# Gated linear attention of the prompt: eight levels of masked pair products in place of sixteen lags and chunk states

## What is computed

```python
def gla_chunked(q, k, v, glog, s0):
    c = math.gcd(q.shape[1], GLA_CHUNK)
    causal = jnp.tril(jnp.ones((c, c), bool))[:, :, None]
    def step(S, inp):
        qc, kc, vc, gc = inp
        bcum = jnp.cumsum(gc, axis=2)
        diff = jnp.where(causal, bcum[:, :, :, None, :] - bcum[:, :, None, :, :], -jnp.inf)
        att = jnp.einsum('bhid,bhjd,bhijd->bhij', qc, kc, jnp.exp(diff))
        o = (jnp.einsum('bhij,bhjv->bhiv', att, vc)
             + jnp.einsum('bhid,bhdv->bhiv', qc * jnp.exp(bcum), S))
        b_last = bcum[:, :, -1:, :]
        S = (jnp.exp(b_last[:, :, 0, :, None]) * S
             + jnp.einsum('bhjd,bhjv->bhdv', kc * jnp.exp(b_last - bcum), vc))
        return S, o
```

## Time and profile before

| | us |
|---|---|
| median of 3 runs | 2249.26 |
| lowest, highest | 2247.94, 2251.69 |
| the profiled execution, its own time | 2248.67 |
| its span, first to last instruction | 2246.9 |
| mean granted TensorE clock | 0.893 |

### The profile page before, as it was taken

One profiled execution on the slowest core, in us unless ns is written; L12 is line 12 of the kernel. 1 busy time (PEld: TensorE's weight loads), 2 busy tenths in 40 slices (PEclk: granted clock), 3 DMA queues, 4 the chain that ended last, 5 costly groups with the idle time before them and its releaser, 6 DMA issues.

```text
span 2246.9 us, 26096 instructions
## 1 busy us (share of the span) xinstructions
PE 1998.4 (89%) x9816; PEld 1517.5 (68%) x9816; DVE 1487.3 (66%) x1522; ACT 996.3 (44%) x1033; POOL 254.4 (11%) x191
## 2 busy tenths in 40 slices
PE   5998678889998984787789999999999999999998
PEld 2784235679996752354667777777777778777776
DVE  1298463445554894534368788787877868788786
ACT  1211311234422213201057666676666667666664
POOL 1159400000002495000000000000000000000000
PEclk9895686799999966865879999999999999999999
DMA  9468473155507691441249899897997979899892
GB/s 366 173 256 291 187 263 123 60 166 180 181 19 283 232 360 38 188 161 67 75 160 362 299 341 341 300 355 293 341 343 284 357 279 355 298 347 345 290 365 110
DMA packets 238516, 552.21 MB, mean 246 GB/s; under 512 B 14792, under 2 KB 43632, under 8 KB 234096
## 3 DMA queue, kind: packets, MB, share of 16 engines
q1 hardware_dynamic: 224736, 475.96, 59.1%
q0 software_dynamic: 5920, 70.23, 8.0%
q10 hardware_dynamic: 7792, 5.08, 0.7%
HBM read 546.16 MB, written 5.08 MB: 245 GB/s over the span
## 4 chain that ended last, share of the span: by engine, by line
PE 46%; DVE 6%; issue 5%; ACT 3%; DVEq 0%; ACTq 0%
PE bank L787 12%; PE bank L789 11%; PE bank L788 11%; DVE WL L1628 2%; ACT WH L1532 2%; PE bank L755 2%; PE bank L1154 2%; PE bank L1076 1%; PE bank L1252 1%; PE bank L813 1%; PE bank L780 1%; PE bank L1006 1%; PE bank L978 0%; DVE Y L2098 0%; PE bank L805 0%
## 5 line engine op out<-in xcount | busy, mean ns | idle before, releaser
L1628 DVE TENSOR_TENSOR WL<-ring_low,WH 128x2048 fp32r<-128x2048 f32 x369 | 838.7, 2290 | 277.8 <-ACT WH L1532 195.2
L1532 ACT ACTIVATE WH<-ring_low 128x2048 fp32r<-128x2048 f32 x336 | 637.9, 1917 | 259.7 <-PE bank L789 259.7
L787 PE MATMUL bank<-WH,HGH 128*128 128x512 f32 x896 | 369.3, 412 | 16.3 <-DVE WL L1628 16.3
L789 PE MATMUL bank<-WH,HGL 128*128 128x512 f32 x896 | 350.5, 391 | 0.0
L788 PE MATMUL bank<-WL,HGH 128*128 128x512 f32 x896 | 349.9, 391 | 0.0
L787 PEld LDWEIGHTS bank<-WH,HGH 128*128 128x128 f32 x896 | 168.7, 188 | 59.7 <-DVE WL L1628 23.4
L787 PE MATMUL bank<-WH,ATH 128*128 128x512 f32 x448 | 186.8, 417 | 24.4 <-DVE ATL L1628 24.4
L789 PEld LDWEIGHTS bank<-WH,HGL 128*128 128x128 f32 x896 | 168.5, 188 | 36.6
L788 PEld LDWEIGHTS bank<-WL,HGH 128*128 128x128 f32 x896 | 168.9, 189 | 32.3
L788 PE MATMUL bank<-WL,ATH 128*128 128x512 f32 x448 | 181.4, 405 | 0.0
L789 PE MATMUL bank<-WH,ATL 128*128 128x512 f32 x448 | 180.8, 404 | 0.0
(11 more groups left out here) (364 smaller groups left out, 2819.5 us busy)
## 6 DMA issues: line engine op xcount, KB each, us to landing
ring_low<-moe_w SPq DMA_DIRECT2D x336, 1024.0 KB, 6.3
ring_low<-ffn_w SPq DMA_DIRECT2D x33, 1024.0 KB, 5.3
ring_low<-w_ada SPq DMA_DIRECT2D x16, 2048.0 KB, 15.3
ring_high<-w_ada SPq DMA_DIRECT2D x8, 2048.0 KB, 16.5
ring_low<-w_in SPq DMA_DIRECT2D x7, 2048.0 KB, 17.5
ring_low<-w_out SPq DMA_DIRECT2D x4, 2048.0 KB, 11.2
ring_high<-w_in SPq DMA_DIRECT2D x3, 2048.0 KB, 8.6
C<-consts SPq DMA_DIRECT2D x1, 1174.0 KB, 18.4
```

The source lines that it names most:

```text
L787: mm(out, sh, mh, start=start, stop=False)
L789: return mm(out, sl, mh, start=False, stop=stop)
L1532: A(WH[:, q % NSPLIT, :], eraw[q % NRAW], ACT.Copy).then_inc(high_ready, 1)
L1628: return tt_(out, full, high.bitcast(F32), ALU.subtract)
```

## The change

The prompt's GLA has no chunks any more. At level n the 256 tokens are taken as blocks of 2^(n+1); a pair (j, i) belongs to the level at which j lies in the left half and i in the right half of the same block. There the decay splits at the middle: the key side takes the gate sum from j to the end of the left half, the query side the sum from the middle to i. So each level needs one scaled copy of all keys and queries (`WX`, half of the tokens as keys, half as queries), and one product of keys with queries per head and tile of 128 tokens (`pair_products`: 8 matmuls with 64 rows and 128 by 128 outputs, half as many at level 7, which joins the two tiles). 0/1 masks keep the level's pairs: DVE copies the product into `ATT` where the mask is one (`keep_pairs`, two predicated copies a level). The pairs i = j come from `gd`, the plain product. `GSUM` (in place of the gates) is extended level by level: after level n the right half adds the left half's sum. It replaces the scan. The factor 1/16 moves into the exponentials' scale.

After level 7 the values meet the pair weights in 12 matmuls (`gy`), read by ACT into `O`. The end state is one token-major product of decayed keys and values (`gtk`, `gst`); values are turned before the levels (`gtv`). All of `VX`, the chunk states, their reads and the additions to `O` are gone.

The fills change: 'lag' is 14 and 8 steps before each of 8 levels (7 and 4 before each of 16 lags), 'kq' 8 and 8, 'gk' 8 and 16; 'vx' and 'states' are gone. The order of background steps is as before, so steps not placed here come in later fills. The core of the diff; a line of "..." also stands where lines of the kernel before, shown above, are taken out:

```diff
-CH = 16
-NCH = NP // CH
+LEVELS = 8
+LMASK = 7
...
+    j, i = np.arange(P)[:, None], np.arange(P)[None, :]
+    masks = [(j >> n + 1 == i >> n + 1) & (j >> n & 1 == 0) & (i >> n & 1 == 1) for n in range(LMASK)] + [i == j]
+    put('levels', np.ascontiguousarray(np.stack(masks, 1).astype(np.uint8)).reshape(P, -1).view(f))
...
-JOBS += [('gate0', 'v'), ('gate1', 'v')] + [(f'att{i}', 'v') for i in range(CH)]
-JOBS += [('gkv0', 'a'), ('gkv1', 'a'), ('gts', 'a')]
-JOBS += [(f'kv{_tt}{_pr}', 'v') for _tt in range(2) for _pr in range(2)]
-JOBS += [('gi0', 'v'), ('gi1', 'v'), ('gx0', 'v'), ('gx1', 'v'), ('gs0', 'v'), ('gs1', 'v'),
+JOBS += [('gate0', 'v'), ('gate1', 'v'), ('gtv0', 'a'), ('gtv1', 'a'), ('gts', 'a'), ('gd0', 'v'), ('gd1', 'v')]
+JOBS += [(f'lv{_n}{_s}', 'v') for _n in range(LMASK) for _s in range(2)]
+JOBS += [('lv70', 'a'), ('lv71', 'a')] + [(f'gy{_h}', 'a') for _h in range(NH)] + [('gtk0', 'a'), ('gtk1', 'a'), ('gst', 'a')]
+JOBS += [('gx0', 'v'), ('gx1', 'v'), ('gs0', 'v'), ('gs1', 'v'),
...
-        'sumb': (8, 0), 'mean': (8, 0), 'var': (0, 0), 'gate': (4, 0), 'lag': (7, 4), 'kq': (3, 7),
-        'vx': (8, 16), 'states': (8, 8), 'gx': (5, 8), 'gs': (4, 0), 'gn': (8, 9), 'rr': (0, 16),
+        'sumb': (8, 0), 'mean': (8, 0), 'var': (0, 0), 'gate': (4, 0), 'lag': (14, 8), 'kq': (8, 8),
+        'gk': (8, 16), 'gx': (5, 8), 'gs': (4, 0), 'gn': (8, 9), 'rr': (0, 16),
...
                 for tt in range(2):
...
+                    token_major(l, f'gtv{tt}', tt, (gv[:, 0, :], gv[:, 1, :]))
                 b = open_job(l, 'gts')
                 for n, src in enumerate((gk[:, 0, NP:T], gk[:, 1, NP:T], gv[:, 0, NP:T], gv[:, 1, NP:T])):
                     ins = turn(b[0:NS, n * P:(n + 1) * P], src, P)
                 close(ins)
+                def pair_products(name, keys, queries, tiles):
+                    for s in range(2):
+                        r = slice(s * HD, (s + 1) * HD)
+                        b = open_job(l, f'{name}{s}')
+                        for n, (kt, qt) in enumerate(tiles):
+                            for c in range(2):
+                                o = (2 * n + c) * P
+                                ins = mm(b[:, o:o + P], keys[r, c, kt * P:(kt + 1) * P],
+                                         queries[r, c, qt * P:(qt + 1) * P], start=True, stop=True)
+                        close(ins)
+                pe.wait_ge(ev["gla_q"], l + 1)
+                pair_products('gd', gk, gq, ((0, 0), (1, 1)))
+                for n in range(LEVELS):
+                    fill('lag')
+                    pe.wait_ge(ev["level_w"], l * LEVELS + n + 1)
+                    pair_products(f'lv{n}', WX[n % 2], WX[n % 2], ((0, 0), (1, 1)) if n < LMASK else ((0, 1),))
+                fill('kq')
+                for name in (f'lv{LMASK - 1}1', 'lv71'):
+                    who, count = read_no(l, name)
+                    pe.wait_ge(job_read[who], count)
+                for h in range(NH):
+                    c, s = h // 2, h % 2
+                    v = [TMV[:, tt, h * HD:(h + 1) * HD] for tt in range(2)]
+                    o = open_job(l, f'gy{h}')[s * HD:(s + 1) * HD, :]
+                    mm(o[:, 0:P], v[0], ATT[:, s, 0, c, :], start=True, stop=True)
+                    mm(o[:, P:NP], v[0], ATT_OFF[:, s, c, :], start=True, stop=False)
+                    close(mm(o[:, P:NP], v[1], ATT[:, s, 1, c, :], start=False, stop=True))
+                fill('gk')
+                pe.wait_ge(ev["gla_kq"], l + 1)
                 for tt in range(2):
...
+                    token_major(l, f'gtk{tt}', tt, (GKD[:, 0, :], GKD[:, 1, :]))
+                b = open_job(l, 'gst')
+                who, count = read_no(l, 'gtk1')
+                pe.wait_ge(job_read[who], count)
+                for h in range(NH):
+                    c, s = h // 2, (h % 2) * HD
+                    for tt in range(2):
+                        ins = mm(b[s:s + HD, c * HD:(c + 1) * HD], TMK[:, tt, h * HD:(h + 1) * HD],
+                                 TMV[:, tt, h * HD:(h + 1) * HD], start=(tt == 0), stop=(tt == 1))
+                close(ins)
...
+                A(GX[:, :, NP:T], GX[:, :, NP:T], ACT.Exp, scale=1.0 / 16.0).then_inc(ev["gla_decays"], 1)
                 for tt in range(2):
...
+                    read(A(TMV[:, tt, :], job(l, f'gtv{tt}')[:, 0:GW], ACT.Copy))
                 read(A(KV8[:, :], job(l, 'gts')[0:NS, :], ACT.Copy))
...
+                for n in range(LEVELS):
+                    rows(l, f'lv{n}1')
+                    act.wait_ge(ev["level_diff"], l * LEVELS + n + 1)
+                    e, g = halves(EX[n % 2], n), halves(GSUM, n)
+                    A(e[:, :, :, 0, :], e[:, :, :, 0, :], ACT.Exp, scale=1.0 / 16.0).then_inc(ev["level_exp"], 1)
+                    A(e[:, :, :, 1, :], g[:, :, :, 1, :], ACT.Exp, scale=1.0 / 16.0).then_inc(ev["level_exp"], 1)
+                act.wait_ge(ev["gla_kd"], l + 1)
+                A(GKD, GKD, ACT.Exp, scale=1.0 / 16.0).then_inc(ev["gla_kexp"], 1)
+                for s in range(2):
+                    read(A(ATT_OFF[:, s].rearrange("p c i -> p (c i)"), job(l, f'lv7{s}')[:, 0:NP], ACT.Copy))
+                for h in range(NH):
+                    c, s = h // 2, (h % 2) * HD
+                    read(A(O[s:s + HD, c, 0:NP], job(l, f'gy{h}')[s:s + HD, 0:NP], ACT.Copy))
+                for tt in range(2):
+                    read(A(TMK[:, tt, :], job(l, f'gtk{tt}')[:, 0:GW], ACT.Copy))
+                read(A(PT[:, P:2 * P], job(l, 'gst')[:, 0:P], ACT.Copy))
+                wait_read(l, 'gst')
+                store(act, gla_out[l, :, :, 0:HD], PT[:, P:2 * P].rearrange("p (c v) -> p c v", c=2))
...
+                signal(tt_(GX, GM, GA, ALU.subtract), "gla_b", l + 1)
                 gq = Z[:, ZT['gq']:ZT['gq'] + 2, :]
                 gk = Z[:, ZT['gk']:ZT['gk'] + 2, :]
...
                 wait_z(l, 'gv')
...
+                signal(ts(gq, gq, HD ** -0.5, None, ALU.mult), "gla_q", l + 1)
+                d.add(V.memset(ATT.rearrange("p s t c i -> p (s t c i)"), 0.0))
+                def difference(n):
+                    g = halves(GSUM, n)
+                    tt_(halves(EX[n % 2], n)[:, :, :, 0, :], bend(block_sum(n), 1 << n), g[:, :, :, 0, :],
+                        ALU.subtract).then_inc(ev["level_diff"], 1)
+                def weights(n):
+                    e, w = halves(EX[n % 2], n), halves(WX[n % 2], n)
+                    if n >= 2:
+                        dve.wait_ge(job_done, job_no(l, f'lv{n - 2}1') + 1)
+                    dve.wait_ge(ev["level_exp"], 2 * (l * LEVELS + n) + 2)
+                    d.add(tt_(w[:, :, :, 0, :], e[:, :, :, 0, :], halves(gk[:, :, 0:NP], n)[:, :, :, 0, :], ALU.mult))
+                    tt_(w[:, :, :, 1, :], e[:, :, :, 1, :], halves(gq[:, :, 0:NP], n)[:, :, :, 1, :],
+                        ALU.mult).then_inc(ev["level_w"], 1)
+                    d.wait()
+                    g = halves(GSUM, n)
+                    d(tt_(g[:, :, :, 1, :], g[:, :, :, 1, :], bend(block_sum(n), 1 << n), ALU.add))
+                def keep_pairs(name, n):
+                    mask = c_('levels', P, n * P // 4, (n + 1) * P // 4).bitcast(U8)
+                    for s in range(2):
+                        read(l, f'{name}{s}', V.copy_predicated(
+                            ATT[:, s].rearrange("p t c i -> p (t c) i"), bmid(mask, 4),
+                            job(l, f'{name}{s}')[:, :].rearrange("p (n i) -> p n i", n=4)))
+                for n in range(LEVELS):
+                    difference(n)
+                    if n == 1:
+                        d.wait()
+                        keep_pairs('gd', LMASK)
+                    elif n >= 2:
+                        keep_pairs(f'lv{n - 2}', n - 2)
+                    weights(n)
+                dve.wait_ge(k_stored, 16 * (l + 1))
+                signal(tt_(GKD, bend(GSUM[:, :, NP - 1], NP), GSUM, ALU.subtract), "gla_kd", l + 1)
+                keep_pairs(f'lv{LMASK - 1}', LMASK - 1)
+                dve.wait_ge(ev["gla_kexp"], l + 1)
+                signal(tt_(GKD, GKD, gk[:, :, 0:NP], ALU.mult), "gla_kq", l + 1)
+                wait_act_read(l, 'gts')
+                dve.wait_ge(job_done, job_no(l, 'lv71') + 1)
                 dve.wait_ge(ev["gla_decays"], l + 1)
...
                 dve.wait_ge(ev["gate_silu"], 3 * (l + 1))
+                wait_act_read(l, 'gy3')
```

More of the change, by code:

```diff
@@ L23 @@
 U32 = mybir.dt.uint32
+U8 = mybir.dt.uint8
 ALU = mybir.AluOpType
@@ L86 @@
                ('cos', T), ('sin', T),
-               ('reset', NP), ('slot', P), ('decay', NH * NP), ('causal', 3 * P),
-               ('chunk', 8), ('half', 2), ('dk', 2 * NH), ('gamma', 2), ('eio', NE)):
+               ('levels', (LMASK + 1) * P // 4), ('slot', P), ('decay', NH * NP), ('causal', 3 * P),
+               ('half', 2), ('dk', 2 * NH), ('gamma', 2), ('eio', NE)):
     CCOL[_k] = (_n, _w)
@@ L246, in host_constants @@
     put('causal', np.concatenate([tri, np.zeros((P, P), f), tri], 1))
```

(63 more changed lines are left out.)

89 lines of the change are left out of this document (10 added, 79 removed).

## The result

The changed kernel takes 2185.48 us (median of 4 runs, 2183.92 to 2187.88) against 2249.03 for the kernel before (4 runs): a ratio of 0.9717, 95% interval 0.9700 to 0.9734. It is 2.8% faster, where 2260, about 11 us slower, was forecast. The profiled execution's span is 2182.1 us, against 2246.9.

A forecast was written before the change was run, and what follows sets the result against it. PE's serial queue of weight-row fills and pair products bounds both stretches. Mostly at 1.2 GHz, layer 0 gives 0, layer 1 -3, later steps -9, overlap +1: about 11 us slower, 2260 us, range 2198 to 2280.

The forecast's parts named there:

- What bounds the stretches: In each layer's gated-attention stretch, PE's serial queue of fills and pair products sets the pace (91.4 and 104.0 us before).
- PE's bank: Sign inside the levels: DVE's idle time in the changed profile would be named after this; no size given.
- the 2.4 us behind ACT's row work: At a row's end, copy, exponentials, weights and hand-overs delay the next products by 2.4 us, with PE idle.
- The price of a set, P: Eight pair-product matmuls of one level on PE: 2.5 us at the full clock, 4.5 at the lower one.
- the isolated row: Trace row L1040, taken as the price of one pair-product matmul: 0.31 us at full clock, 0.56 at the lower.
- The twelve products with the values: PE matmuls behind the levels, priced at 12 x 0.56 = 6.7 us at the lower clock.
- The clock: Both stretches mostly at 1.2 GHz: layer 1 nearly all through, layer 0 a third of the time at 2.4.
- the first rival: Full clock holds in both stretches, 64-row matmuls counting like 128-row ones: 2200 us, faster; chance 0.24.
- Later steps: Weight-row steps issued later, behind the stretches: 5 us lost in layer 0, 4 in layer 1; 3 each at full clock.
- Layer 0 alone (2239): Only layer 0, with its long value fills, gets the full clock: 10 us faster, 2239; chance 0.10.
- slow copies: Predicated copies in the levels above 4 us each make DVE pass PE; at 5 us each, 2277; chance 0.05.
- no change: Something else, the weight rows or pages, paces the stretches, so shortening them changes nothing: 2249; chance 0.04.

The follow-up runs named there:

- the same half twice: Both jobs of each set of pair products read partitions 0 to 63, against the changed kernel; 2218.03 us.
- half the steps: Weight-row steps ahead of each level cut from 14 to 7 in layer 0 and 8 to 4 in layer 1, against the changed kernel; 2185.78 us.
- the pair of serial kernels: Changed kernel with both jobs of each set reading partitions 0 to 63 (2218.03 us), or all 128 partitions (2174.32 us).

## Why the prediction was wrong

**What bounds the stretches**: right in the main. PE's queue did, but not it alone: DVE's idle time inside the levels stands against ACT's exponentials (L1443, 21.0 us in layer 0 behind level 0), and not against PE's bank as I had named for a sign; ACT was held by row work that waited for PE, and PE lost 5.2 and 3.6 us to it. DVE's level took 3.0 us for the 3.2 forecast, a predicated copy 0.74 for 0.72, PE's wait for the row copy 0.70 to 0.77 for 0.74, and the 2.4 us behind ACT's row work shows as 2.33 in level 1 of layer 0, behind a turn; in the layer's other levels the wait was at most 0.89. Doubling the copies changed no more than the scatter.

**The price of a set, P**: wrong, and the first of two failed steps. 4.5 and 2.5 us were forecast, 3.03 and 1.64 measured. Two causes, told apart by the run with the same half twice: 0.8 and 0.5 of it was the isolated row taken for a matmul in a run of eight, 0.7 and 0.3 the overlap of the halves. The forecast called PE's queue "strictly serial" and gave the overlap 1 us for the whole kernel ("may overlap a little at their seams"). The twelve products with the values, three for one column half and then three for the other, took 1.7 us in both layers at the upper clock (323.71 to 325.44 in layer 0), for 3.7 forecast; their overlap was not tested by itself. Over a layer, nine sets took 18.1 and 18.9 us; at the forecast prices and the same clocks they would be some 9 longer, and the value products 2: 11 in each layer.

**The clock**: wrong, the second failed step and the larger. I forecast a third of layer 0 at 2.4 GHz and almost nothing of layer 1. A mean of 0.78 and 0.77 means that 56% and 54% of the time was granted 2.4 GHz, and as twice the work is done there, 0.72 and 0.70 of the work. Put into the prediction's own sums, that gives 102.9 - 0.72 x 34.5 = 78.1 us in layer 0 and 110.4 - 0.70 x 38.4 = 83.5 in layer 1. Less the 11 above it is 67 and 72.5, against 65.7 and 70.3 measured. So the sum's structure held. Against the forecast's shares (1/3, and 3 of 38.4, 0.08, in layer 1) the clock makes 0.39 x 34.5 = 13 and 0.62 x 38.4 = 24 us, the prices 22: 59, where the two stretches came out 63 shorter than forecast (91.4 + 107.4 = 198.8 against 136.0); the 4 that are missing are about those by which the sums above lie too high. That the forecast weighted by time and not by work was an error of its own: a third of the time at 2.4 GHz is half of the work, so 6 of layer 0's 13 us.

The reading behind the clock was not wrong in kind. Rows of 64 do count for less: the kernel with the same half twice did in layer 1 what was forecast, a clock of 0.53. (The forecast also counted layer 1's turns with the matmuls of 64 rows, as 6.3 of 12.5 us; the earlier trace rows show them with 128.) Its stretch of 95.9 us is the forecast's 110.4, less 8.5 sets x 0.8, less 3.5 for the twelve value products (3.2 us there for 6.7), less 0.11 x 38.4 for the small share at the upper clock: 95.9. So in layer 1 what the forecast missed is the overlap itself: take it away, and the clock is gone as well as the price. In layer 0 it is not. There the serial kernel still got 0.76, which is 0.68 of the work, so 12 of the 13 us by which the forecast missed that layer's clock have nothing to do with the overlap. Beyond the 6 us of the weighting their cause stays open. The fall to 0.66 with half the steps points to the long full-row fills, of which I had expected less. The scores of FoX, on which I leaned, are mostly 4-row matmuls; the text named that as the point for the first rival, and it should have weighed more.

**Later steps**: forecast 5 and 4 us lost. Layer 0's gain of 25.7, with 2.0 ahead of the stretch that are scatter of its start, has shrunk to 24.2 by the start of the next stretch (892.75 to 868.58): 3.5 lost, near the forecast. Layer 1 was wrong in sign: its output projection starts 64.7 us earlier (L1076 at 1070.96, now 1006.23), 6.8 more than the stretch's end. The clock had been 0.57 over the 74 us behind the stretch before and was 0.70 over the same work now, with the extra full-row steps in it; that these steps raised it was not tested.

**The rivals**: the first, 2200 us by a clock that holds, was the right side and the nearest, 15 us too high. Its reason, that a matmul of 64 rows does as well as one of 128, is what the pair of serial kernels disproves; its clock came halfway true, and its serial prices were too high by 22. That it came near is luck in part. Layer 0 alone (2239), slow copies and no change are out by the same traces.

## What to carry to other kernels

Before pricing matmuls of 64 rows, look at which half each neighbour reads. Serial ones cost as much as full ones, and in one of the two layers here they took the clock down to 0.53; alternating ones cost little more than half (1.09 against 1.98 us a set). And where the clock is in play, an estimate of an edit's own microseconds is too small: here one edit moved the time by 33 us where its own matmuls make 6 to 12, and another by 22 where the waits that it removed make 8. Work put into idle time needs a look at what it will itself wait for.

## What was not expected of the hardware

- With the same matmuls in number and order, the granted clock over layer 1's stretch was 0.53 with 64 rows filled and 0.94 with 128, at 91% and 84% busy; over layer 0's, 0.76 and 0.92.
- Eight fp32 matmuls of 64 rows and 128 columns take 1.98 us (2.4 GHz) in one half, 1.64 as four and four, 1.09 alternating; at 1.2 GHz 3.71, 3.03 and 2.01.
- The same matmul is dearer alone between others (0.56 us at 1.2 GHz) than in a run of eight (0.46).
- A predicated copy of 512 elements, mask of bytes, source in a bank, takes 0.74 us, 0.06 more than a plain operation of that size.
